# Two layers written out, next rows turned amid last products, hidden rows used two steps late, casts and sigmoids reordered

## The reference

```python
# first block, DEPTH = 2, D_FF = 2816
h = rmsnorm(x, norm_mix)
proj = h @ w_in                     # three attentions and the gates
o_a, o_b, o_c = swa_sink_attention(...), stick_breaking_attention(...), moba_attention(...)
g = sigmoid(gates + b_gate)
merged = sum(g[:, :, i] * (o_i @ w_branch[i]))
x = x + merged @ w_out
h = rmsnorm(x, norm_ffn)
u = causal_depthwise_conv(h @ w_up, conv_w, conv_b)      # width 3
u_a, u_v = split(u, 2)
x = x + (silu(u_a) * u_v) @ w_down
# second block, layer 0 dense (2816), layer 1 of 8 experts (3584), top 2
x = layer_norm(ALPHA * x + hybrid_mixer(x))
x = layer_norm(ALPHA * x + (swiglu(x) or moe_swiglu(x)))
```

## Time and profile before

| | us |
|---|---|
| median of 3 runs (2582.46 to 2585.60) | 2584.82 |
| the profiled execution | 2584.39 |
| its span from first to last instruction | 2582.8 |
| TensorE busy in it | 2450.2 |
| VectorE, ScalarE busy | 1869.3, 1443.5 |
| first two layers | 0 to 966 |
| experts | 1561 to 2552 |

### The profile page before, as it was taken

The page is one execution under the profiler, slowest core; times in us unless marked ns, Lnnn a source line. Parts: engine busy times, 40 slices in busy tenths (PEclk is TensorE's granted clock), DMA queues, the critical chain, the costliest instruction groups (busy, mean ns, idle before and its releaser), DMA issues.

```text
span 2582.8 us, 37086 instructions
## 1 busy us (share of the span) xinstructions
PE 2450.2 (95%) x13300; PEld 2069.1 (80%) x13300; DVE 1869.3 (72%) x2118; ACT 1443.5 (56%) x1433; POOL 61.7 (2%) x75
## 2 busy tenths in 40 slices
PE   9999899899999999999999989999999999999995
PEld 8877799797778988679988667777777787878784
DVE  4666798656668876554466457888888888888887
ACT  5565444355653435333435236777777777777773
POOL 0100000000000000000000001000000000000000
PEclk9999999999999999699999689999999999999997
DMA  7335455343455544247544128999999999999996
GB/s 277 136 131 180 165 197 193 139 157 123 171 181 183 178 180 163 90 155 237 194 147 150 63 82 338 369 349 367 355 363 364 358 377 352 373 351 375 361 373 243
DMA packets 93873, 616.05 MB, mean 239 GB/s; under 512 B 9776, under 2 KB 17600, under 8 KB 22464
## 3 DMA queue, kind: packets, MB, share of 16 engines
q1 hardware_dynamic: 88544, 591.51, 62.2%
q0 software_dynamic: 5216, 23.04, 2.4%
HBM read 599.30 MB, written 15.20 MB: 238 GB/s over the span
## 4 chain that ended last, share of the span: by engine, by line
PE 61%; issue 22%; DVE 8%; ACT 5%; DVEq 3%; POOL 1%; ACTq 1%; DMA 0%; POOLq 0%; SPq 0%
PE bank L315 18%; PE bank L317 18%; PE bank L316 18%; DVE w_lo L611 4%; ACT w_hi L523 3%; PE bank L429 2%; DVEq L603 2%; DVE probs L672 1%; PE bank L1745 1%; PE bank L439 1%; POOL probs L783 1%; DVE x_tok L2159 0%; PE bank L454 0%; ACT probs L564 0%; DVE arena L1416 0%
## 5 line engine op out<-in xcount | busy, mean ns | idle before, releaser
L611 DVE TENSOR_TENSOR w_lo<-raw,w_hi 128x2048 fp32r<-128x2048 f32 x550 | 1252.4, 2296 | 397.5 <-ACT w_hi L523 375.9
L523 ACT CAST w_hi<-raw 128x2048 fp32r<-128x2048 f32 x550 | 1049.9, 1913 | 449.3 <-PE bank L317 430.0
L315 PE MATMUL bank<-w_hi,hT_hi 128*128 128x512 f32 (+3 forms) x1296 | 517.5, 399 | 17.6 <-DVE w_lo L611 13.9
L317 PE MATMUL bank<-w_hi,hT_lo 128*128 128x512 f32 (+3 forms) x1296 | 502.7, 388 | 0.0
L316 PE MATMUL bank<-w_lo,hT_hi 128*128 128x512 f32 (+3 forms) x1296 | 502.6, 388 | 0.0
L315 PE MATMUL bank<-hT_hi,w_hi 128*128 128x256 f32 (+1 forms) x1568 | 451.1, 288 | 13.9 <-DVEq L634 12.1
L317 PE MATMUL bank<-hT_hi,w_lo 128*128 128x256 f32 (+1 forms) x1568 | 446.0, 284 | 0.0
L316 PE MATMUL bank<-hT_lo,w_hi 128*128 128x256 f32 (+1 forms) x1568 | 446.0, 284 | 0.0
L315 PE MATMUL bank<-w_hi,oT_hi 128*128 128x512 f32 x940 | 373.2, 397 | 28.9 <-DVE oT_lo L2334 11.2
L316 PE MATMUL bank<-w_lo,oT_hi 128*128 128x512 f32 x940 | 369.1, 393 | 0.0
L317 PE MATMUL bank<-w_hi,oT_lo 128*128 128x512 f32 x940 | 368.5, 392 | 0.0
(11 more groups left out here) (288 smaller groups left out, 1668.0 us busy)
## 6 DMA issues: line engine op xcount, KB each, us to landing
raw<-in_weights_dram SPq DMA_DIRECT2D x554, 1024.0 KB, 6.7
token_rows<-all_cols SPq DMA_DIRECT2D x11, 512.0 KB, 7.2
arena<-in_norms_dram POOLq DMA_DIRECT2D x2, 2048.0 KB, 8.0
nat<-token_rows POOLq DMA_DIRECT2D x8, 512.0 KB, 7.9
unit_rows<-probs POOLq DMA_DIRECT2D x8, 512.0 KB, 8.8
arena<-in_b_gate_dram POOLq DMA_DIRECT2D x6, 512.0 KB, 4.4
unit_rows<-all_cols SPq DMA_DIRECT2D x4, 512.0 KB, 9.7
tables<-in_tables_b_dram POOLq DMA_DIRECT2D x1, 1216.0 KB, 5.7
```

Of the source, the lines that this page charges most:

```text
L315: mm(out, st[0], mv[0], start=start, stop=False, skip_group_check=True)
L317: return mm(out, st[1], mv[0], start=False, stop=stop, skip_group_check=True)
L523: self.isa.copy(m.w_hi[:, slot, :], m.raw[:, raw, :]).then_inc(m.hi_ready, 1)
L611: self.isa.tensor_tensor(m.w_lo[:, slot, :], m.raw[:, raw, :], m.w_hi[:, slot, :].bitcast(F32), ALU.subtract).then_inc(m.lo_ready, 1)
```

## The change

The layers of the first block are written out: each engine's loop becomes `for layer in range(DEPTH)` over its text, the columns are read from `all_cols` and their copy goes. While the last down product of a layer runs, TensorE turns the first half of the next layer's rows, between its two k tiles of the second half; VectorE subtracts that half right after it has added it, so the next layer starts without turning. In the first block's feed-forward, hidden rows are multiplied two steps after their up products, from three places instead of two, and the chunks are laid out in that order; VectorE and ScalarE handle fewer chunks in steps 1 and 2. The row factors are spread between the two second-half products. In the projection three k tiles go ahead of the turning instead of two; four casts go ahead of the squares, and the squares of half 1 ahead of its turned rows. With the stick heads the last weighing uses bank 3, and two exponentials go ahead of two casts of results. In the softmax the sigmoids of the gates stand behind the third copy of the probabilities and the first cast of results. In the experts the last two steps are rearranged: the next rows are turned before `rows_down(5)`, the last hidden rows between the two chunks of it, and they have places of their own (`LAST_HIDDEN`); ScalarE is three casts ahead of the y rows, which it copies with `copy` instead of an activation. The loops' count tables of the layers go too.

```diff
+    def cols(self, layer, at, n):
+
+        return self.all_cols[:, layer * A_PARAMS + at:layer * A_PARAMS + at + n]
...
 class TensorA(Tensor):
-    def layer(self):
+    def layer(self, layer):
         m, w = self.m, self.w
         ident, rot = m.tab(A_TABLES, "ident"), m.tab(A_TABLES, "rot64")
-        self.eng.wait_ge(m.shared_loaded, 16)
-        self.eng.wait_ge(m.x_half, w.next(m.x_half))
-        self.turn_half(m.x, 0, (0, 1), ident)
+        if layer == 0:
+            self.eng.wait_ge(m.shared_loaded, 16)
+            self.eng.wait_ge(m.x_half, w.next(m.x_half))
+            self.turn_half(m.x, 0, (0, 1), ident)
         self.two_by_halves([self.bank(b) for _, _, b in STICK_IN[0:2]], m.x, (2, 3), ident)
...
-        self.two_by_halves([self.bank(0), self.bank(1)], m.x, (2, 3), ident)
-        self.spread_roots(2, ident)
-        self.feed_forward_a()
-
-    def two_by_halves(self, banks, src, turn_banks, ident):
+        self.two_by_halves([self.bank(0), self.bank(1)], m.x, (2, 3), ident, 2)
+        self.feed_forward_a(layer, ident)
...
-        for bank, c in zip(banks, chunks):
+        for i, (bank, c) in enumerate(zip(banks, chunks)):
+            if i and roots is not None:
+                self.spread_roots(roots, ident)
...
-                    self.rows(banks, c, 512, merged, kt, k0, KT, ks=(0, 2))
+                    self.rows(banks, c, 512, merged, kt, k0, KT, ks=(0, 3))
                     self.eng.wait_ge(m.nat_ready, self.w.next(m.nat_ready))
                     self.turn_half(m.nat, 1, (2, 3), ident)
-                    last = self.rows(banks, c, 512, merged, kt, k0, KT, ks=(2, 4))
+                    last = self.rows(banks, c, 512, merged, kt, k0, KT, ks=(3, 4))
...
-    def down_a(self, j):
-        m = self.m
-        p = j % 2
+    def down_a(self, j, turn=None):
+
+        m = self.m
+        p = j % 3
         self.eng.wait_ge(m.hid_ready, self.w.next(m.hid_ready))
         if j == 0:
             for b in (4, 5, 6, 7):
                 self.bank(b)
-        c = self.chunk()
+        c, total = self.chunk(), 2 if j == FF_SUBS - 1 else 3
         hid = (m.oT_hi[:, 2 * p:2 * p + 2, :], m.oT_lo[:, 2 * p:2 * p + 2, :])
-        for half in range(2):
-            last = self.rows([m.bank[4 + 2 * half], m.bank[5 + 2 * half]], c, D, hid, 2, 0,
-                             2 if j == FF_SUBS - 1 else 3, col=512 * half, opened=j > 0)
-            if half == 0 and j == FF_SUBS - 1:
-                last.then_inc(m.to_dve[4], 1)
+        last = self.rows([m.bank[4], m.bank[5]], c, D, hid, 2, 0, total, opened=j > 0)
+        if j == FF_SUBS - 1:
+            last.then_inc(m.to_dve[4], 1)
+        for k in range(2):
+            last = self.rows([m.bank[6], m.bank[7]], c, D, hid, 2, 0, total, col=512, opened=j > 0, ks=(k, k + 1))
+            if turn and k == 0:
+                turn()
         self.used(last)
-    def feed_forward_a(self):
+    def feed_forward_a(self, layer, ident):
+
+        m = self.m
+
+        def next_layer():
+            self.eng.wait_ge(m.x_half, self.w.next(m.x_half))
+            self.turn_half(m.x, 0, (0, 1), ident)
         for j in range(1, FF_SUBS):
             self.up(j % 2)
-            self.down_a(j - 1)
-        self.down_a(FF_SUBS - 1)
+            if j >= 2:
+                self.down_a(j - 2)
+        self.down_a(FF_SUBS - 2)
+        self.down_a(FF_SUBS - 1, next_layer if layer + 1 < DEPTH else None)
...
-        def out(h):
-            self.weigh_pair(h, lambda h: [a_v(m, t, P + h * DH, P + (h + 1) * DH) for t in range(TT)], 4)
+        def out(h, b=4):
+            self.weigh_pair(h, lambda h: [a_v(m, t, P + h * DH, P + (h + 1) * DH) for t in range(TT)], b)
...
-        out(6)
+        out(6, 3)
...
 class ScalarA(Scalar):
-    def layer(self):
-        m = self.m
-        self.eng.wait_ge(m.cols_ready, self.w.next(m.cols_ready))
-        self.turned_half(0, (0, 1), m.hT_hi, NORM_MIX)
+    def layer(self, layer):
+        m, w = self.m, self.w
+        self.turned_half(0, (0, 1), m.hT_hi, m.cols(layer, NORM_MIX, 4))
         self.split(1)
         self.squares((0,))
-        self.turned_half(1, (2, 3), m.hT_hi, NORM_MIX)
+        self.turned_half(1, (2, 3), m.hT_hi, m.cols(layer, NORM_MIX + 4, 4))
         self.squares((1,))
         self.split(4)
         self.split(2)
-        self.eng.wait_ge(m.rstd, self.w.next(m.rstd))
+        self.eng.wait_ge(m.rstd, w.next(m.rstd))
         self.inputs_out(STICK_IN[4])
         self.stick_beside_inputs(4)
         self.softmax_beside(0, True)
@@ -1074,30 +1086,23 @@
         self.gates(1)
         self.split(2)
         self.turned_half(0, (0, 1), m.oT_hi)
-        self.split(1)
+        self.split(2)
         self.gates(1)
-        self.split(1)
         self.turned_half(1, (2, 3), m.oT_hi)
+        self.split(4)
+        self.squares((0,))
+        self.turned_half(0, (0, 1), m.hT_hi, m.cols(layer, NORM_FFN, 4))
         self.split(2)
-        self.squares((0,))
-        self.split(1)
-        self.turned_half(0, (0, 1), m.hT_hi, NORM_FFN)
-        self.split(3)
-        self.turned_half(1, (2, 3), m.hT_hi, NORM_FFN)
         self.squares((1,))
-        w = self.w
+        self.turned_half(1, (2, 3), m.hT_hi, m.cols(layer, NORM_FFN + 4, 4))
         self.eng.wait_ge(m.rstd, w.next(m.rstd))
-        self.split(2)
-        self.hidden(0)
-        for j in range(1, FF_SUBS):
-            self.split(2)
-            self.hidden(j % 2, 1)
-
-    def turned_half(self, half, banks, hi, norm=None):
-        m = self.m
-        tiles = range(4 * half, 4 * half + 4)
-        scales = None if norm is None else m.cols[:, norm + 4 * half:norm + 4 * half + 4]
-        self.high_turned(banks, hi, scales, tiles)
+        for j in range(FF_SUBS):
+            self.split(1 if j in (1, 2) else 2)
+            self.hidden(j % 3, 1)
+        self.split(1)
...
-        self.oT_high(5, tile0, (4, 4))
         weights(6)
         weights(7)
-        self.oT_high(7, tile0, (4, 4))
+        self.oT_high(5, tile0, (4, 3))
+        self.oT_high(7, tile0, (4, 3))
...
-        self.gates()
         self.split(1)
         self.probs_out(2, 2)
         self.oT_high(1, tile0, (3, 3))
+        self.gates()
...
 class VectorA(Vector):
     def layer(self, layer):
         m, w = self.m, self.w
-        self.isa.tensor_copy(m.cols[:, 0:A_PARAMS], m.all_cols[:, bass.ds(layer * A_PARAMS, A_PARAMS)]) \
-            .then_inc(m.cols_ready, 1)
-        sinks = m.cols[:, SINKS:SINKS + 8]
+        self.layer_now = layer
+        sinks = m.cols(layer, SINKS, 8)
         cos, sin = m.tab(A_TABLES, "cos64"), m.tab(A_TABLES, "sin64")
-        self.low_half(0, (0, 1), m.hT_hi, m.hT_lo, NORM_MIX)
-        self.split(1)
-        self.low_half(1, (2, 3), m.hT_hi, m.hT_lo, NORM_MIX)
+        if layer == 0:
+            self.low_half(0, (0, 1), m.hT_hi, m.hT_lo, m.cols(layer, NORM_MIX, 4))
+        self.split(1)
+        self.low_half(1, (2, 3), m.hT_hi, m.hT_lo, m.cols(layer, NORM_MIX + 4, 4))
         self.mean_squares(D, 1e-6)
         self.split(2)
         self.eng.wait_ge(m.shared_loaded, 16)
@@ -1285,20 +1290,24 @@
         self.eng.drain().then_inc(m.nat_ready, 1)
         self.low_half(1, (2, 3), m.oT_hi, m.oT_lo)
         self.eng.wait_ge(m.probs_turned, w.all_free(m.probs_turned))
-        self.split(2)
-        self.add_half(0)
-        self.split(1)
-        self.low_half(0, (0, 1), m.hT_hi, m.hT_lo, NORM_FFN)
-        self.split(2)
-        self.add_half(1)
-        self.split(1)
-        self.low_half(1, (2, 3), m.hT_hi, m.hT_lo, NORM_FFN)
+        self.split(3)
+        self.add_half(0, w.product_done())
+        self.split(1)
+        self.low_half(0, (0, 1), m.hT_hi, m.hT_lo, m.cols(layer, NORM_FFN, 4))
+        self.split(1)
+        self.add_half(1, w.product_done(-1))
+        self.split(1)
         self.mean_squares(D, 1e-6)
+        self.low_half(1, (2, 3), m.hT_hi, m.hT_lo, m.cols(layer, NORM_FFN + 4, 4))
         self.eng.wait_ge(m.rstd, w.next(m.rstd))
         for j in range(FF_SUBS):
-            self.hidden(j % 2, j, 1 if j else 0)
-        self.add_half(0, True)
-        self.add_half(1)
+            self.split(0 if j in (1, 2) else 1)
+            self.hidden(j % 2, j, 1)
+        self.split(1)
+        self.add_half(0)
+        if layer + 1 < DEPTH:
+            self.low_half(0, (0, 1), m.hT_hi, m.hT_lo, m.cols(layer + 1, NORM_MIX, 4))
+        self.add_half(1, w.product_done(-1))
...
-    def add_half(self, half, within_chunk=False):
-
-        m = self.m
-        if within_chunk:
+    def add_half(self, half, products=None):
+
+        m = self.m
+        if products is None:
             self.eng.wait_ge(m.to_dve[4], self.w.next(m.to_dve[4]))
         else:
-            self.eng.wait_ge(m.w_used, self.w.product_done(-1))
+            self.eng.wait_ge(m.w_used, products)
...
+        s = j % 3
         for b, dst, half in ((2 * p, gate, 0), (2 * p + 1, value, 1)):
-            self.split(1)
+            self.split(half)
...
```

(57 more changed lines are left out.)

54 lines of the change are left out of this document (20 added, 34 removed).

## The result

The changed kernel takes 2535.69 us (median of 6 runs, 2534.92 to 2539.20) beside 2583.64 of the kernel before: a ratio of 0.9815, 95% interval 0.9801 to 0.9830. It is faster by 48 us, 1.9%, clear of the noise; 2530 within 2512 to 2552 was forecast. The profiled executions are 2584.39 and 2539.20, 45.2 apart, where the sum had 55.6.

What follows compares the result with a forecast made beforehand. TensorE was taken as the bound, busy 2450.2 of 2582.8 us, with waits and low-clock stretches to win. Savings of 39.1 us, 55.6 with the clock, took 2584.4 to 2528.8, stated as 2530, range 2512 to 2552.

Steps and rivals of the forecast that it cites:

- (i): Granted clock in the first two layers and experts: shorter waits remove three quarters of the slow stretches' 22.1 us, 16.5 saved.
- (b): Softmax: moving the sigmoids of the gates clears four waits for probsT, 7.5 us, plus 0.5 for a follower; 8.0 saved.
- (h): Experts, eight units: rearranged unit ends cut waits from 3.6 to 2.85 us and drop a fourth stop; 6.2 us saved.
- (g): Turn of the layers: TensorE's 7.5 us wait mostly goes, with rows turned amid the last down product; 7.0 us saved.
- (a): Start of the kernel: the copy of the columns and ScalarE's table load go; 1.7 us saved.
- (d): Wait on L1285 for the second half of the merged rows: three k tiles ahead instead of two save 2.0 us.
- (e): Projection and second half: casts ahead of squares save 4.6 us, roots between two products 1.0.
- (f): First layers' feed-forward: hidden rows used two steps late remove 10.0 us of waits, new w_lo waits return 3.6; net 6.4.
- Rival B: Clock stays low: slow stretches move to other places, the clock term gives only 2 us; 2543 us, chance 0.18.
- C: ScalarE and VectorE bind at reordered places: nothing from experts, 4 instead of 1.8 us a feed-forward layer; 2545, chance 0.12.
- D: Experts: the table load at the unit loop's head goes too, about 2 us a turn; 2514 us, chance 0.09.
- E: Slower: engines stop for instructions in the written-out layers, some 3 us per stop; 2595 us, chance 0.04.

## Why the prediction was right, and where it was off

The direction and the range hold, and so does the mechanism: waits that were named with their releaser went, and most of the slow clock with them. The largest term, (i), came out at its size, the second, (b), at half. Against the sum (55.6, with 45.2 measured) 4.0 are missing in (b), 2.8 in (h), 1.4 in (g), and 3.2 were taken back by the middle. Step by step, by the waits of the layers:

- (a) 1.7 forecast; the first product stands at 14.41 us in place of 16.21: 1.8, and the wait before it is 1.7 in place of 3.2 us. No table load stands there any more. The start itself moves by some 0.5 us between executions of the same text (13.8 to 14.8).
- (b) 8.0 forecast, 4.0 measured: 7.5 us of waits for probsT became 3.5 for oT_lo. The step that failed is "clears them": VectorE's subtraction of a chunk and then of oT_lo is late right behind ScalarE. The runs put 3 us on the move of the sigmoids. Writing the layers out alone took 2.2 of the 7.5 and added 1.9 for oT_lo.
- (c) 2.2 forecast, 2.1 measured. (d) 2.0 and 2.3.
- (e) and (f): 5.6 + 6.4 = 12.0 forecast, 12.1 measured (w_lo 11.3 to 4.3, L1492 3.9 to 0, the tables 1.2 to 0). The new waits for w_lo in the feed-forward that VectorE's pace predicted, 1.0 and 0.8 a layer, are there with 0.81 and 0.51. The shares are others, though: undone alone, (e) with (d) costs 10.5, where 7.6 was worked out, and (f) 4.6, where 6.4 was. The order of the projection also decides how far VectorE is ahead when the feed-forward starts, as the three stops more in each layer show, and the forecast priced the two apart.
- (g) 7.0 forecast, 5.6 measured. "About 0.4 remains" missed that a list of both banks is asked for ahead of the first product, and that bank 6 is emptied by the add of half 1, which VectorE now does after the turned rows. This was in the order of the code, not in the trace of before.
- (h) 6.2 forecast without the clock. The waits went from 25.1 to 17.0 us, 1.0 a unit as worked out, but a unit became only 0.6 shorter (123.6 to 123.0). The other 0.4 came back as products that start further apart; at each wait the last product before it and the first behind it take some 0.27 us more together, and there is one wait more. The experts gave 7.0 us with the clock; three slow stretches of 1.2 went there, so (h) by itself is 3.4.
- (i) 16.5 forecast. More than three quarters went (44.2 to 3.4 us), and each us of it was worth less than the half that was assumed. A stretch is full of products only in part. At the low clock products of 512 columns start 0.43 us apart in place of 0.23, those of 256 columns 0.21 (18.10 and 18.31) in place of 0.12 (22.00 and 22.12); a stretch of 3.41 us full of them costs 1.6 or 1.5 us:

```profile
478.05 0.40 PE L315 MATMUL bank<-w_hi,oT_hi 128*128 128x512 f32 x1
478.29 0.39 PE L316 MATMUL bank<-w_lo,oT_hi 128*128 128x512 f32 x1
...
479.58 0.63 PE L317 MATMUL bank<-w_hi,oT_lo 128*128 128x512 f32 x1
480.00 0.63 PE L315 MATMUL bank<-w_hi,oT_hi 128*128 128x512 f32 x1
```

  In the experts of the kernel before, the second, third and sixth unit, each with a stretch, take 124.8 us and the fourth, fifth and seventh, without one, 123.6, so 1.2 comes through. In the layers, 41.2 us less the 27.9 of waits leaves 13.3 for 30.6 us of slow clock, 0.43 for each. That makes 16.9 in all, by subtraction. The forecast was met because two errors, in the share that goes and in its price, nearly cancel. Its rule was too simple too: two of the eleven stretches (the earlier trace rows gives only the longest of the four waits for probsT) stood behind waits of 1.7 us, not of 2 or more, and two waits of 1.9 and 2.0 had none.
- The middle was taken as unchanged. It varies by 10 us by itself.

Rival B is out: no stretch moved to another place in the layers or the experts of the changed kernel. C is out: the waits for VectorE in the feed-forward are 2.6 us in both layers together, not 4 a layer. D didn't happen, for the reason that was given against it, and the Silu ahead of the loop shows its price: 18 us in the stretch of the experts (from chunk 215 on 993.6 in place of 1012.0), 16 forecast. E is out by the run that was written out only, and it went the other way.

What turned out larger than forecast is the loop. The first two layers written out are worth 15 to 18 us alone, a third of the whole. Beside the branch and the loads, the waits inside a loop are reckoned with registers. In the first two layers of the kernel before the trace has 466 register operations on TensorE's queue, 298 on ScalarE's and 310 on VectorE's; written out there are none, and 194, 200 and 58 semaphore instructions stand there in place of 38, 46 and 14. VectorE's stops of issue ahead of L669, in the first layer of the kernel before and of the written-out one:

```profile
DVE small L669 <- issue: 4.6, 15, 0.7
```
```profile
DVE small L669 <- issue: 2.5, 13, 0.2
```

That without these operations the waits for probsT are shorter, and through them the slow clock, fits and is argued, not shown: no run has the loop without its registers.

The trace does not show the drain of about 1380 ns that the Trainium skill ("ScalarE: Activation LUTs", What ACT_TABLE_LOAD costs) has beside the load of a table: a load takes 1.28 us, and where ScalarE's next instruction has no wait it starts 0.02 later. That a unit became 2.55 us shorter without its two loads doesn't bear on this, since TensorE then no longer waits there.

## What to carry over

A table load at the head of a loop means that the table on entry differs from the one at the loop's end: one tiny activation ahead of the loop took it away and gave 15 us to the kernel before and 20 to the changed one. When TensorE is the bound, look first for its longest waits, since a slow stretch behind one costs 1.2 to 1.5 us more, and price a stretch by how far apart its products start. (A count of the products that touch a stretch takes in those that only end in it.) An edit ahead of a stage can change how far the engines are ahead when it starts, so undo edits one at a time before giving each its share. A list of banks asked for ahead of the first product waits for the last of them.

## What the runs showed of the hardware

- TensorE's clock fell to 0.50 (1.2 GHz) behind four of four waits of 2.5 to 3.0 us for probsT and behind none of the same four at 1.0 to 1.5. But one wait does not always do it. In the fourteen traces, outside the middle and after the first 5 us, none of 79 waits of 1.2 to 1.6 us has a stretch behind it, 21 of 63 of 1.7 to 2.2 have one, and 14 of 16 longer ones; each stretch stands behind a wait of 1.7 or more. In the run that was only written out, the wait before the second step of the feed-forward (3.1 us) has a stretch in the first layer (at 310 us) and none in the second, and the 2.9 at the turn has none. Of the eight turns of a unit in the kernel before, with waits of 1.4 and 1.94 us each, three had one.
- The changed kernel differs by 10 us from one execution to the next on the same chip (2529.5 to 2540.1), and between the two that were profiled, of 2529.5 and 2539.2 us, the clock of the middle accounts for the difference: 585.3 us at 0.90, 595.2 at 0.88.
